# Order of the first loads of a hybrid decoder layer: token tiles ahead of the key weights

## The reference

```python
h = _rmsnorm(x, g_pre_mix)
proj = h @ w_in.astype(x.dtype)
u_pool, q, k, v, o_pre, i_pre, f_pre, gate_pre = jnp.split(proj, split_idx, axis=-1)
...
C_new = decay[..., None, None] * C + jnp.einsum('bhj,bhjd,bhje->bhde', wk, k, v)
```

## Time and profile before

| | us |
|---|---|
| median of 3 runs | 2731.56 |
| lowest and highest of them | 2680.68, 2770.17 |
| the profiled execution, its time | 2670.8 |
| its span on the slowest core (core 6) | 2669.3 |
| spans of all 8 cores | 2638.2 to 2669.3 |
| PE busy in the span | 2414.4 (90%) |
| DVE, ACT, POOL busy | 786.3, 508.8, 324.6 |
| mean granted TensorE clock of the cores | 0.958 to 0.965 |

### The profile page before, as it was taken

The page is one execution under the profiler, slowest core; times in us unless marked ns, Lnnn a source line. Parts: engine busy times, 40 slices in busy tenths (PEclk is TensorE's granted clock), DMA queues, the critical chain, the costliest instruction groups (busy, mean ns, idle before and its releaser), DMA issues.

```text
span 2669.3 us, 51016 instructions; the slowest of 8 cores (2638.2 to 2669.3 us)
## 1 busy us (share of the span) xinstructions
PE 2414.4 (90%) x18175; PEld 1489.9 (56%) x18175; DVE 786.3 (29%) x1513; ACT 508.8 (19%) x949; POOL 324.6 (12%) x497
## 2 busy tenths in 40 slices
PE   3999999999899999998769999999989999984389
PEld 3756874785454444455445555555555666652245
DVE  2552136126551121114552222222222000022434
ACT  4321024114231111114331000000000111111211
POOL 1000115114310000005430000000000000000000
PEclk9999999999899999999889999999999999996689
DMA  8232704772854455644555777777785544546676
GB/s 210 96 58 35 117 18 72 120 121 33 145 98 69 78 95 84 105 68 101 133 128 101 155 171 190 178 183 174 188 180 157 105 95 93 109 115 177 209 172 188
DMA packets 137452, 328.62 MB, mean 123 GB/s; under 512 B 14258, under 2 KB 80818, under 8 KB 123826
## 3 DMA queue, kind: packets, MB, share of 16 engines
q0 software_dynamic: 40144, 163.66, 37.5%
q1 hardware_dynamic: 97058, 161.71, 19.3%
HBM read 416.55 MB, written 72.42 MB: 183 GB/s over the span
## 4 chain that ended last, share of the span: by engine, by line
PE 80%; DMA 12%; DVE 3%; issue 2%; ACT 1%; SPq 1%; POOL 1%; DVEq 0%; ACTq 0%; POOLq 0%
PE ps L138 79%; DMA x2s<-big 4%; DMA CS<-big 2%; DMA big<-sC 2%; DVE big L183 2%; DMA big<-xT 1%; DMA big<-x 1%; DVE big L162 1%; PE ps L142 1%; SPq L135 1%; DMA big<-x1s 1%; DMA big<-wu_t 1%; POOL big L162 0%; ACT big L159 0%; DMA big<-wq_t 0%
## 5 line engine op out<-in xcount | busy, mean ns | idle before, releaser
L138 PE MATMUL ps<-big 128*128 128x368 bf16 (+8 forms) x17696 | 2392.5, 296 | 196.4 <-DVE big L162 107.7
L138 PEld LDWEIGHTS ps<-big 128*128 128x128 bf16 (+2 forms) x17696 | 1459.3, 99 | 1108.2 <-issue 286.5
L159 ACT ACTIVATE big<-ps 128x368 f32<-128x368 f32 (+4 forms) x411 | 196.3, 478 | 1128.6 <-PE ps L138 1103.8
L162 DVE TENSOR_TENSOR big<-big,ps 128x368 bf16<-128x368 f32 (+6 forms) x284 | 147.8, 522 | 835.4 <-PE ps L138 767.2
L162 DVE TENSOR_TENSOR big<-big 128x368 f32<-128x368 f32 (+13 forms) x362 | 192.4, 532 | 398.2 <-ACT big L159 285.1
L162 POOL TENSOR_TENSOR big<-big 128x1 f32<-128x1 f32 (+5 forms) x207 | 172.7, 839 | 207.5 <-ACT big L159 188.1
L183 DVE SCALAR_TENSOR_TENSOR big<-big,ps 128x1024 f32<-128x1024 f32 (+1 forms) x128 | 129.3, 1010 | 101.3 <-PE ps L138 60.4
L183 DVE SCALAR_TENSOR_TENSOR big<-big 128x368 f32<-128x368 f32 (+5 forms) x160 | 112.5, 725 | 48.6 <-DMA big<-fsc 41.2
L159 ACT ACTIVATE big<-big 128x368 f32<-128x368 f32 (+7 forms) x110 | 72.6, 661 | 161.9 <-DVE big L162 117.6
L135 POOL DMA_DIRECT2D big<-wgu_t x44 | 23.5, 534 | 587.1 <-PE ps L138 568.3
L187 ACT COPY big<-ps 128x368 f32<-128x368 f32 (+2 forms) x100 | 45.7, 457 | 251.8 <-PE ps L138 247.6
(11 more groups left out here) (37 smaller groups left out, 280.0 us busy)
## 6 DMA issues: line engine op xcount, KB each, us to landing
big<-wgu_t POOLq DMA_DIRECT2D x44, 1024.0 KB, 11.0
big<-sC SPq DMA_DIRECT2D x64, 512.0 KB, 5.4
CS<-big SPq DMA_DIRECT2D x64, 512.0 KB, 7.2
big<-wmg_t POOLq DMA_DIRECT2D x16, 1792.0 KB, 15.0
big<-wdn_t POOLq DMA_DIRECT2D x16, 1408.0 KB, 11.2
big<-x SPq DMA_DIRECT2D x16, 1024.0 KB, 6.5
big<-sC POOLq DMA_DIRECT2D x64, 256.0 KB, 6.1
big<-wpg_t POOLq DMA_DIRECT2D x16, 576.0 KB, 9.0
```

The source lines that it names most:

```text
L138: return self.add("pe", lambda e: e.matmul(out, lhsT, rhs, start=start, stop=stop, **kw), w=[out], r=[lhsT, rhs])
L159: return self.add(eng, lambda e: e.activation(out, in_, func, **kw), w=w, r=r)
L162: return self.add(eng, lambda e: e.tensor_tensor(out, in0, in1, op), w=[out], r=[in0, in1])
```

## The change

The first token tile is issued on SP ahead of the constants, and tiles 1 and 2 between the constants and `ghT`. The four quarters of the key weights are no longer issued at the start: quarters 0, 1, 2 and 3 are issued on POOL inside `xprep(i)` for i = 0, 2, 4 and 6, behind the two POOL instructions of `xstat(i)` and so behind the landing of tile i; the gate weights likewise for i = 5. `xload`, `xst` and `rows` move up in the file. `NDMA_Q["act"]` becomes 8 (no DMA is issued from ACT).

```diff
--- before.py
+++ after.py
@@ -9,7 +9,7 @@
 
 ENGS = ("pe", "act", "dve", "pool", "sp")
 NDMASEM = 12
-NDMA_Q = {"pool": 8, "sp": 12, "act": 4, "pe": 4, "dve": 4}
+NDMA_Q = {"pool": 8, "sp": 12, "act": 8, "pe": 4, "dve": 4}
 _DSZ = {F32: 4, BF16: 2, mybir.dt.int32: 4, mybir.dt.uint8: 1}
 
 def _dsize(dt):
@@ -506,8 +506,17 @@
         def w2(dst, src):
             S.dma("pool", dst, src)
 
+        xst = [A.view(o_R4 + i * 8192, [128, DM], F32) for i in range(3)]
+        rows = [(i * 128, 128) for i in range(16)] + [(2048, 64)]
+
+        def xload(i):
+            r0, n = rows[i]
+            S.dma("sp", xst[i % 3][0:n, :], x[r0:r0 + n, :])
+
+        xload(0)
         S.dma("sp", csb, cst)
-        S.dma("pool", wg.rearrange("p a b -> p (a b)"), wig_t)
+        xload(1)
+        xload(2)
         S.dma("sp", ghT, ghT_in)
         S.copy("dve", identB, identF)
         S.memset("dve", onesF, 1.0)
@@ -521,18 +530,11 @@
         PB = Bump(A, o_R5, o_END)
         hTP = PB.alloc([128, 16, NPFX], BF16)
         kP = PB.alloc([128, 8, 1024], BF16)
-        xst = [A.view(o_R4 + i * 8192, [128, DM], F32) for i in range(3)]
         xbf = [A.view(o_R3 + i * 4096, [128, DM], BF16) for i in range(2)]
         xjk = A.view(o_R3 + 8192, [128, DM], BF16)
         gbuf = A.view(o_R4 + 24576, [128, 9, 32], F32)
         pgst = A.view(o_R4 + 24576 + 1152, [128, 8, 4], F32)
         psTs = [ps[:, i * 1024:(i + 1) * 1024].bitcast(BF16).rearrange("p (a b) -> p a b", a=16) for i in range(2)]
-        rows = [(i * 128, 128) for i in range(16)] + [(2048, 64)]
-
-        def xload(i):
-            r0, n = rows[i]
-            S.dma("sp", xst[i % 3][0:n, :], x[r0:r0 + n, :])
-
         def run(g):
             for _ in g:
                 pass
@@ -561,6 +563,10 @@
         def xprep(i):
             if i < 17:
                 xstat(i)
+            if i in (0, 2, 4, 6):
+                w2(wkq[i // 2].rearrange("p a b -> p (a b)"), wk_t[i // 2])
+            if i == 5:
+                w2(wg.rearrange("p a b -> p (a b)"), wig_t)
             if 1 <= i <= 17:
                 xscale(i - 1)
 
@@ -576,11 +582,6 @@
                 c0 = HALO + (i - 8) * 128
                 dst = hT[:, :, c0:c0 + n]
             S.tt("dve", dst, pT[:, :, 0:n], gT.unsqueeze(2).broadcast_to([128, 16, n]), ALU.mult)
-
-        for i in range(3):
-            xload(i)
-        for q in range(4):
-            w2(wkq[q].rearrange("p a b -> p (a b)"), wk_t[q])
 
         pbK = itertools.cycle((4, 5, 6))
         done = {"g": False}
```

## The result

The changed kernel takes 2663.2 us in the median (15 runs), the kernel before 2680.68 (15 runs, the three shown above among them). The ratio of the two is 0.9942, 95% interval 0.9925 to 0.9959: faster by 15.5 us, with 11 to 20 in the interval. (Of the three runs shown before, 2731.56 and 2770.17 had one die slowed down, which comparisons leave out.) A second comparison on another chip (experiment e5) gave 0.9949, 0.9930 to 0.9968: 13.6 us. The forecast was 14.0 us less, but put as 2718 us and as "no change that can be told". That the size was near is in part luck: the place where the gain was to arise gave 8.1 to 9.3 us, as the rest of this text shows.

The account below looks back on a forecast made before the run. TensorE bounds most of the kernel, but the front waits for token tiles sharing full DMA engines with key weights. Lead-in 17.1 us earlier, some 3 given back: 14.0 off 2670.8 gives 2656.8, off the median 2731.56 gives 2718; range 2650 to 2746.

Parts of the forecast that it names:

- no change that can be told: Verdict on the whole time: a measurement tells about 2% (55 us) from no change; same 0.91, faster 0.05, slower 0.04.
- The gate weights, quarters 2 and 3, and GpSimd's issues are hidden: Key stage: these weights land before TensorE wants them, quarter 3 with 25 us of slack; five GpSimd issues cost nothing.
- That DVE could hold up GpSimd's issues: Moved quarter issues: a quarter might start one DVE instruction later; sum unmoved, quarters 1 to 3 having 9 us and more.
- The carry to the end in full: Behind the front: no later wait absorbs the gain, so all 14.0 us count through to the end.
- no cost: Constants behind tile 0: they land some 3 us late, but their only early user, the identity, is needed after 14.
- tile 0 lands at 6.0, tile 1 at 10.2: Start of the front: tile 0 lands at 6.0 us (before: 14.67), then the constants, and tile 1 at 10.2.
- its data start 1.5 later: Tile 3, issued at 14.3 us: data from about 16.0, shared with quarters 0 and 1, landing at 25.3.
- the walk: Tile-by-tile timing of the front: key projection's lead-in at 29.5 us, tile 5's transposes at 51.4 instead of 65.37.
- the lower bound of 8: Least gain, 8 us: tiles 3 to 6 all at the shared pace, tile 5's transposes at 57.3.
- Hidden anyway: Rival, 2728 to 2735 us: the gain is used up at the next wait; chance 0.10.
- Slower: Rival, 2749 us: TensorE works at its slow clock among the front's gaps; chance 0.04.
- More: Rival, about 2704 us: the DMA engines keep the tiles ahead, gain 24 to 30; chance 0.06.

Follow-up runs that it names:

- e3: Changed kernel without the staggering: tile 0 first, but gate weights and all four quarters issued at the start; 1.0002 of the kernel before.
- e11: As e1, but quarters 1, 2, 3 only behind the squares of tiles 6, 8, 10, gate weights behind tile 7; 2677.65 us in a single run.
- e7: As e1, plus a fourth buffer for token tiles 0 to 7, so tile 3 is issued at the start; 0.9955 of the kernel before.
- e10: As e7, but quarters 1, 2, 3 behind the squares of tiles 3, 5, 7, gate weights behind tile 6; 0.9948 of the kernel before.
- e4: As e1, but quarters 1, 2, 3 behind the squares of tiles 3, 5, 7, gate weights behind tile 6; 0.9986 of the kernel before.
- e1: Changed kernel with one edit: DVE clears the accumulators ssz before it copies the identity; 0.9962 of the kernel before.
- e6: As e1, but quarter 0 issued at the start behind tile 0, without waiting for its squares; 0.9956 of the kernel before.
- e2: Changed kernel with the constants issued first again, then tiles 0, 1, 2, quarters still staggered; 0.9975 of the kernel before.
- e9: As e1, but each quarter issued as four transfers of four kc each instead of one; 0.9940 of the kernel before.

## Why the prediction was right or wrong

**What can be told.** The step that failed first is the sentence that a measurement of this kernel tells about 2% from no change. I took the spread of the three runs shown for its resolution and gave "no change" 0.91. The runs that are compared agree within 0.4 to 0.6%, and the ratio has an interval of plus or minus 0.17%. The kernel against itself gave 1.0002, plus or minus 0.0012. So a forecast of 14 us was a forecast of "faster", by 0.5%, and should have been written as one.

**The level.** The working gave 2656.8 on the profiled execution; measured 2662.55, and 2663.2 in the median. I moved it to the median of the three, 2731.56, and that made 2718. The profiled execution and the lowest of the three lay within 10 us of each other and the other two 51 and more above: that pair was the level, and the range of 2650 to 2746 held the result only because I had kept its low end.

**Where the chain was right.** The front was the place: e3 shows that the whole effect is the removal of the weights' share beside the first tiles. The gate weights, quarters 2 and 3, and GpSimd's issues are hidden, as said; no core of the changed kernel waits for a quarter, and in the variants only e11 does for long (10.5 to 13.3 us; e7 and e10 at most 2.3). That DVE could hold up GpSimd's issues changed nothing that was to be seen: on core 7 they took 0.60 to 0.73 us each. The clock, at a granted 0.50 behind the pause, cost 1.7 us on core 7 of the changed kernel, 1.9 on core 2 of e4 and 3 on core 5 of e7. The carry to the end in full holds within what is measured, best seen in the mean of cores.

**The constants, "no cost".** Wrong in the reading: I named the identity as the only early user and overlooked the memset behind its copy in DVE's stream, on which ACT's first squares wait. It made the squares of tile 0 start at 10.6 instead of 7.3, of which taking the gate away brings back 1.9. Its price in the stage is 0.5 (e1).

**The first tiles, "tile 0 lands at 6.0, tile 1 at 10.2".** The first mis-sized term. I gave tile 0 the shortest landing in the whole trace, 4.8 us; it took 6.2, and tile 1 landed at 12.3, 2.1 late. That puts the issue of tile 3 at 16.6 instead of 14.3, with the gate or without it (16.4 in e1).

**Tile 3, "its data start 1.5 later".** The second mis-sized term. I took the lag of a transfer that meets idle engines. Tile 3 meets a quarter that already has them, and its first packets moved 4.1 to 4.4 us after the issue on the late cores, 3.4 to 3.6 on the early ones; into idle engines, in e6, it was 0.9 to 2.4. In the kernel before, the tiles had been queued since 2 us, so the rows of before show only the shared pace of 9.3 and never this wait. In the mean of cores tile 3 lands at 29.8 instead of 25.3: 2.3 us from its late issue, 2.1 from the wait, 0.1 from the pace. That is the 4.5 us by which tile 2's transposes came late. On core 7 it is 33.25, with 2.7, 2.4 and 2.8. The four cores that end early issued tile 3 at 15.8 to 16.4, the four late ones at 16.8 to 17.2, and in e5 it is the same (15.9 to 16.3 against 16.9 to 17.1). It isn't that microsecond alone: in e2 the issues overlap (16.0 to 16.6 on the early cores, 16.5 to 17.6 on the late), and what differs is the wait, 3.2 to 3.8 against 4.4 to 5.0. Why it differs by core stays open.

**The same again at tile 6.** On core 7 tile 6 is squared at 54.9 against 47.3 in the walk; it is issued at 41.23, one microsecond behind quarter 2, and its first packet moves at 46.96, 5.7 later. The two give 57.3 for tile 5's transposes in the mean of cores, forecast 51.4, and 8.7 us for the stage, near the lower bound of 8 that I got by giving every tile the shared pace. So the stage gave 8.7 to 9.3 of the 14.0, and totals of 15.5 and 13.6 so near to 14 are luck: the first lies above what the front gave by more than its interval, and the mean of cores gives e5 10.8.

**The rivals.** "Hidden anyway" fell: the gain is in the end time. "Slower" by the clock fell: 1.7 us of it is there. "More" fell.

## What to carry to other kernels

A transfer that is needed next should be issued ahead of the bulk, not just apart from it: a tile issued one to three microseconds behind a quarter paid 3.4 to 5.8 us before its first packet here. Where the packets of two queues go one for one, as they do here, their sizes make the shares: cutting the bulk transfer into narrower rows gave the urgent queue twice the bandwidth, and TensorE never waited for the bulk. A wait ahead of a short burst of TensorE work costs the wait and the slow clock behind it. When the metric is the slowest of 8 cores, read the mean of the cores beside it: it told apart what the metric could not. And a forecast of half a per cent is a forecast of a direction: ask for the resolution of the comparison, not for the range of a few runs.

## What the runs showed of the hardware that I had not expected

- Two cores that are neighbours don't get the same start: in both profiles of the changed kernel one of each pair ends the key stage 2.3 to 6.8 us before the other, and which one changes from run to run. With four buffers (e7) the difference is 1.7 us at most, with the quarters in pieces (e9) 1.6. The early side is a microsecond ahead from its first landing on (tile 0 at 6.2 to 6.7 against 7.8 to 8.5). No run here shows why.
- Four pieces with rows of 2 KB written, in place of one transfer with rows of 8 KB, left the tiles 235 instead of 105 GB/s beside them. The quarters pay for it: the last piece landed up to 18.7 us after its issue on core 7, a whole quarter within 15.7. Both together moved no fewer bytes than before: 1.88 + 2 x 0.49 MB read in 8 us (0.36 MB in a microsecond), against 1.05 + 2 x 1.02 in 10 (0.31).
- A tile issued 1 to 3 us behind a quarter moves nothing for 3.4 to 5.8 us and then at once its full share of packets. Cutting the bulk into pieces did not shorten that (3.4 to 4.7 in e9); with the engines idle it is 0.9 to 2.4 (e6).
- A pause of 2 to 8 us on TensorE was followed by a granted clock of 0.50 on some cores and not on others: in the changed kernel on core 7 behind 2.26 us of idleness, not on core 2 behind 3.23.
